# A hybrid decoder trunk on one core: another order of work in the state-space scans, and of the output projection and the way into the last feed-forward block

## What is computed

```python
proj = u @ w_in                       # z (2048 columns), x/B/C (3072), dt (32)
xbc = silu(causal_depthwise_conv(xbc, conv_w, conv_b))
y = ssd_chunked(xs, dt, A, Bm, Cm) + xs * D       # 4 groups of 8 heads, 8 chunks of 128 tokens
y = y * silu(z)
yg = y.reshape(b, s, 4, 512)
yg = yg * rsqrt(mean(yg * yg, axis=-1) + EPS)     # one RMS norm per group
x = x + (yg.reshape(b, s, 2048) * norm_w) @ w_out
x = x + swiglu(rmsnorm(x, ffn_norm_w[1]), ...)    # silu(h @ w_gate) * (h @ w_up) @ w_down
x = rmsnorm(x, final_norm_w)
```

## Time and profile before

| | |
|---|---|
| median of 3 runs | 2369.83 us (2365.24 to 2371.79) |
| the profiled execution: device time / span | 2368.59 / 2366.9 us |
| PE busy | 2267.5 us (96%) |
| DVE, ACT, POOL busy | 1425.3, 1146.5, 1373.0 us (60, 48, 58%) |
| DMA | 317.16 MB, mean 134 GB/s |
| mean granted TensorE clock | 0.982 of full speed |

### The profile page before, as it was taken

One profiled execution on the slowest core, in us unless ns is written; L12 is line 12 of the kernel. 1 busy time (PEld: TensorE's weight loads), 2 busy tenths in 40 slices (PEclk: granted clock), 3 DMA queues, 4 the chain that ended last, 5 costly groups with the idle time before them and its releaser, 6 DMA issues.

```text
span 2366.9 us, 29286 instructions
## 1 busy us (share of the span) xinstructions
PE 2267.5 (96%) x10602; PEld 1841.8 (78%) x10602; DVE 1425.3 (60%) x1828; ACT 1146.5 (48%) x2101; POOL 1373.0 (58%) x992
## 2 busy tenths in 40 slices
PE   8999999999999999999999889779979999999998
PEld 6876888888888878888777667558768888888887
DVE  7366754333346888745578778658873424335787
ACT  4056643333334447555588767424643333333445
POOL 3234288777765654877344434235568777774654
PEclk9999999999999999999999989889999999999999
DMA  5110233232339653333444534476323233227844
GB/s 158 54 27 19 107 99 119 85 116 85 116 111 329 206 163 116 107 107 117 137 134 134 179 133 143 165 251 187 126 73 121 98 116 116 85 98 248 268 150 157
DMA packets 193787, 317.16 MB, mean 134 GB/s; under 512 B 21696, under 2 KB 106604, under 8 KB 191084
## 3 DMA queue, kind: packets, MB, share of 16 engines
q1 hardware_dynamic: 191212, 307.55, 38.6%
q10 hardware_dynamic: 2432, 7.73, 0.8%
HBM read 230.68 MB, written 84.56 MB: 133 GB/s over the span
## 4 chain that ended last, share of the span: by engine, by line
PE 84%; DVE 7%; DMA 3%; issue 2%; POOL 2%; SPq 1%; ACT 1%; DVEq 0%; ACTq 0%; POOLq 0%
PE ps L2525 42%; PE ps L2228 5%; PE ps L2230 5%; PE ps L2229 5%; PE ps L2617 5%; PE ps L2621 5%; PE ps L2613 5%; PE ps L2909 1%; PE ps L2913 1%; PE ps L2905 1%; PE ps L2251 1%; PE ps L2974 1%; PE ps L2694 1%; DMA bc_rows<-conv_rows 1%; PE ps L2957 1%
## 5 line engine op out<-in xcount | busy, mean ns | idle before, releaser
L1274 POOL TENSOR_TENSOR s_lo<-s_val,s_hi 128x512 fp32r<-128x512 f32 x154 | 236.1, 1539 | 197.3 <-ACT s_hi L1863 196.7
L3279 DVE TENSOR_TENSOR xres<-ps,xres 128x512 f32<-128x512 f32 x132 | 90.6, 688 | 407.5 <-PE ps L2525 407.5
L1172 POOL TENSOR_TENSOR p_lo<-p_val,p_hi 128x512 fp32r<-128x512 f32 x176 | 240.1, 1374 | 48.8 <-ACT p_hi L1616 43.3
L1616 ACT ACTIVATE p_hi<-p_val 128x512 fp32r<-128x512 f32 x176 | 111.0, 632 | 310.8 <-POOL p_val L1202 310.8
L1143 POOL TENSOR_TENSOR w_lo<-w_raw,w_hi 128x1024 fp32r<-128x1024 f32 x34 | 81.5, 2401 | 195.4 <-ACT w_hi L1471 108.7
L2525 PE MATMUL ps<-xn_hi,p_hi 128*128 128x512 f32 x704 | 190.8, 393 | 1.9 <-ACT xres L1765 1.3
L2525 PE MATMUL ps<-xn_lo,p_hi 128*128 128x512 f32 x704 | 188.8, 390 | 1.4 <-DVE xn_lo L3145 1.4
L2525 PE MATMUL ps<-xn_hi,p_lo 128*128 128x512 f32 x704 | 188.2, 389 | 0.0
L1863 ACT ACTIVATE s_hi<-s_val 128x512 fp32r<-128x512 f32 x154 | 96.9, 629 | 149.1 <-DMA d_val<-in_w_down 86.9
L2228 PE MATMUL ps<-xn_hi,w_hi 128*128 128x512 f32 x400 | 162.1, 405 | 0.0
L2229 PE MATMUL ps<-xn_lo,w_hi 128*128 128x512 f32 x400 | 157.2, 393 | 0.0
(11 more groups left out here) (385 smaller groups left out, 5680.0 us busy)
## 6 DMA issues: line engine op xcount, KB each, us to landing
s_val<-hidden SPq DMA_DIRECT2D x154, 256.0 KB, 2.9
hidden<-xres SPq DMA_DIRECT2D x20, 1792.0 KB, 6.5
wv_g<-in_w_gate SPq DMA_DIRECT2D x22, 1024.0 KB, 5.2
wv_u<-in_w_up SPq DMA_DIRECT2D x20, 1024.0 KB, 5.2
d_val<-in_w_down SPq DMA_DIRECT2D x70, 256.0 KB, 4.0
rows_v<-in_w_down SPq DMA_DIRECT2D x64, 256.0 KB, 3.7
mdec<-decay_sums SPq DMA_DIRECT2D x32, 512.0 KB, 3.9
os_val<-gated_y SPq DMA_DIRECT2D x56, 256.0 KB, 2.8
```

The source lines that it names most:

```text
L1172: pool.tensor_tensor(p_lo[n][:, :, :], src, f(p_hi[n][:, :, :]), ALU.subtract).then_inc(p_lo_done, 1)
L1274: pool.tensor_tensor(s_lo[i][:, :], s_val[i][:, :], f(s_hi[i][:, :]), ALU.subtract)\
L1616: act.activation(p_hi[n][:, :, :], src, ACT.Copy).then_inc(p_hi_done, 1)
```

## The change

- **Scans.** On DVE the rests of the group before stand between `masked_decay(c)` and `token_major(k + 1)`, where they stood behind `token_major`; their chunks are others, and the sums of squares come from POOL to DVE (`square_adds`, 3 instructions in place of 3). POOL takes `w_lo` in halves, at places tied to `cb_full`. `root` and `root_row` of half 0 stand in chunk 7 of the same group (before: chunk 0 of the next), those of half 1 in chunk 3 (before: 4). SP issues `load_bc(g + 1, 0)` in chunk 4 or 5 and `load_xrows(g + 1, 0)` in chunk 5 (before: both in 6, behind stores), `load_xrows(g, 1)` in chunk 0 of g itself. SiLU is spread over the chunks 3, 5, 7 and 1. The last group takes z in pairs and then two threes.
- **Projection.** Eleven slices need nothing of the last group's rests (before: nine); of them SP loads slices 0 to 5 within the scans (before: 0 and 1), with `root_row` ahead of `load_out(3)`. The stores and loads behind them are in a new order. The y side's rests of slices 0 and 1 are DVE's, of 2 to 55 POOL's as before. The 16 additions of M1 to x all stand ahead of the rest of slice 16.
- **Into the FFN.** M7's additions, `make`, `second_T` and `lo` come up to three slices earlier, and the parts of the tail are interleaved otherwise.

```diff
-        OUT_SEQ = ([(0, p) for p in range(6)] + [(1, p) for p in range(3)] + [(0, p) for p in (6, 7)]
-                   + [(1, p) for p in range(3, NO)] + [(j, p) for j in range(2, 7) for p in range(NO)])
+        OUT_SEQ = ([(0, p) for p in range(6)] + [(1, p) for p in range(5)] + [(0, p) for p in (6, 7)]
+                   + [(1, p) for p in range(5, NO)] + [(j, p) for j in range(2, 7) for p in range(NO)])
...
-                         [(0, 1, 2), (3, 4), (5, 6), (7, 8), (9, 10), (11, 12, 13), (14, 15), ()]]
-        SILU_AFTER_CHUNK = [{1: (0, 1), 4: (2, 3, 4)}] + [{2: (0, 1), 4: (2, 3), 6: (4, 5)}] * (G - 1)
-        SILU_LATE = [(5, 6, 7)] + [(6, 7)] * (G - 1)
-        NEXT_PIECE = {6: 0, 7: 1}
-        LATE_PIECE = {0: 2, 1: 3}
+                         [(0, 1), (2, 3), (4, 5), (6, 7), (8, 9), (10, 11, 12), (13, 14, 15), ()]]
+        SILU_AFTER_CHUNK = [{1: (0, 1), 3: (2, 3), 5: (4,), 7: (5,)}]
+        SILU_AFTER_CHUNK += [{3: (0, 1), 5: (2, 3), 7: (4, 5)}] * (G - 2) + [{3: (0, 1), 5: (2, 3), 6: (4,), 7: (5,)}]
+        SILU_LATE = [(6, 7)] * G
...
+        LO_AHEAD = [{1: (2, 0), 2: (3, 0)}] + [{0: (0, 1), 1: (1, 0), 2: (2, 0), 3: (3, 0), 4: (3, 1)}] * (G - 1)
+        LO_BEHIND = [{1: (2, 1), 2: (3, 1)}] + [{1: (1, 1), 2: (2, 1)}] * (G - 1)
+        S_LO_DVE = 2
...
+            def half_lo(piece, half):
+                cols = slice(half * BANK, (half + 1) * BANK)
+                pool.wait_ge(hi_done, piece.count(1))
+                ins = pool.tensor_tensor(w_lo[piece.slot][:, cols], raw[piece.raw][:, cols], f(w_hi[piece.slot][:, cols]),
+                                         ALU.subtract)
...
+            def square_adds(n):
+
+                dve.wait_ge(sq_ready, BG * (n + 1))
+                dve.tensor_tensor(sq[0][:, :], sq[0][:, :], sq[1][:, :], ALU.add).then_inc(sq_added, 1)
+                dve.tensor_tensor(sq[2][:, :], sq[2][:, :], sq[3][:, :], ALU.add).then_inc(sq_added, 1)
+                dve.wait_ge(sq_added, 2 * (n + 1))
+                dve.tensor_tensor(sq[0][:, :], sq[0][:, :], sq[2][:, :], ALU.add).then_inc(sq_summed, 1)
...
                     masked_decay(c)
+                    if c == 0 and g:
+                        for b in range(BG):
+                            row_normed(g - 1, b, 0)
+                    if c == 1 and g:
+                        gated(g - 1, 1)
+                    if c == 2 and g:
+                        square_adds(2 * g - 1)
+                        mixes(g - 1, "S1")
+                    if c == 3 and g:
+                        reciprocal_rms(2 * g - 1)
+                    if c == 4 and g:
+                        for b in H1_ORDER:
+                            row_normed(g - 1, b, 1)
+                    if c == 5:
+                        if g:
+                            mixes(g - 1, "S3")
+                        gated(g, 0)
+                    if c == 6:
+                        square_adds(2 * g)
+                        if g:
+                            mixes(g - 1, "S2")
+                    if c == 7:
+                        reciprocal_rms(2 * g)
+                        if g:
+                            mixes(g - 1, "S4")
                     if k + 1 < NT * G:
                         token_major(k + 1)
-                    if c == 0 and g:
-                        gated(g - 1, 1)
-                        reciprocal_rms(2 * g - 2)
-                    if c == 2 and g:
-                        for b in range(BG):
-                            row_normed(g - 1, b, 0)
...
-                        if (j, p) == (1, 7):
-                            quota, limit = 8, "M1"
-                        elif j >= 2 and p in (0, 1):
-                            quota, limit = (4, "M1") if j == 2 else (0, "M1")
+                        if (j, p) in ((1, 6), (1, 7)):
+                            quota, limit = 4 if p == 6 else 12, "M1"
```

More of the change, by code:

```diff
@@ new lines, in ssd_group @@
+                    if c == 5:
+                        if g:
+                            sp.wait_ge(mix_ready, 8 * q + 4)
+                        else:
+                            for i in range(4):
+                                sp.wait_ge(row_stored[i], 16 * ((len(ROWS) - 1 - i) // 4 + 1))
+                            sp.wait_ge(gc_ready, 1)
+                            load_bc(1, 0)
+                        if not last:
+                            load_xrows(g + 1, 0)
+                        if g:
+                            store_blocks(q, "M7")
@@ L1099, in out_loads @@
+                load_out(15)
+                load_x_back(3)
+                load_x_back(7)
+                for s_ in range(16, OUTS):
                     load_out(s_)
@@ L3216, in second_entry @@
                     taken = 0
[L3217 removed]
+                    for s_ in range(10, OUTS):
                         j, p = OUT_SEQ[s_]
@@ L3257, in second_entry @@
                         tail_b22(i)
-                    for i in range(4):
-                        tail_lo1(i)
+                    make(6)
+                    tail(0)
+                    make(7)
+                    tail(1)
+                    tail(2)
+                    tail_lo1(0)
+                    tail_lo1(1)
+                    tail_t1(3)
+                    tail_t2(3)
+                    tail_lo1(2)
+                    tail_lo1(3)
                     for i in range(4):
```

365 lines of the change are left out of this document (186 added, 179 removed).

## The result

The changed kernel takes **2338.28 us** (median of 4 runs, 2336.78 to 2339.91), the kernel before 2367.53 (4 runs, 2364.37 to 2371.79): ratio **0.9875, 95% interval [0.9856, 0.9895]**. That is 29 us less, where 66 were forecast: less time as said, though by 1.25%, and outside of the range. The profiled execution took 2339.18 us, its span is 2337.2.

The account below looks back on a forecast made before the run. PE was taken as the bound, with about 100 us of losses that an order of work can reach. Gains of 29 + 28 + 4 + 5 = 66 us off 2368.6 gave 2303 us, range 2284 to 2328.

Parts of the forecast that it names:

- Term 1: Scans: earlier input loads end the 20.2 us of `bc_rows` waits, `mdec` waits nearly go; gain 29 us of 34.3 lost.
- I keep 5 us: Scans: 5 us of the 34.3 us loss left in place, for the row's tight round trip and POOL's `xds`.
- it fits by 0.7: Scans, chunks 7 and 3: ydiag through row and `row_normed` to the next `mdec` takes 17.7 us against two chunks' 18.4.
- rival (a): Scans: the row comes late in every group, `rr_rows` taking 6.8 us behind bytes; 18 us back, 2321; chance 0.13.
- Term 2: Projection to slice 16: half 1's row chain costs nothing, smaller waits remain; gain 28 us of 41.8 lost, bounds 18 and 36.
- I add 5: Projection: 5 us allowed for DMA, about 16 MB needed by slice 16 taking 45 us, close to PE's 46.4.
- The clock behind two waits: 3: Projection: 3 us allowed for PE's slower clock after two waits.
- Term 3: Slices 16 to 55: earlier `make` and `second_T` take the idle 3.2 us and a little clock; gain 4 us (2 to 5).
- Into the FFN: Way into the FFN: DVE is the bound; `make`, tails and two late ops interleaved save its idle time; gain 5 us (2 to 9).
- Rival (b): Projection: POOL's rests starve at 4.1 us each while DVE works without a break; 19 us back, 2322; chance 0.12.
- (c): Scans: the wait for inputs stays because `load_xrows` waits for S3; 24 us back, 2327; chance 0.06.
- (d): Scans: DVE becomes the bound, about 99 us per group; 2386 us, slower than before; chance 0.05.

Follow-up runs that it names:

- the versions with all edits: Changed kernel with all follow-up edits except late input loads: rests on VectorE 2303.14 us, rests on POOL 2306.76, rests on VectorE with half 1's row first 2301.90.
- the best versions: Changed kernel with all follow-up edits except late input loads, rests on VectorE: 2303.14 us; same with half 1's row before the early x loads: 2301.90 us.
- the single edit: Changed kernel with the y-side rests of slices 2 to 15 on VectorE instead of POOL: 2335.82 us, ratio 0.9856.
- the combination: Changed kernel with all follow-up edits except late input loads: 2303.14 us with the rests of slices 2 to 15 on VectorE, 2306.76 with them on POOL.

## Why the prediction was wrong

- **Term 1, scans, gain 29, was 21.5.** Its mechanism held: the 20.2 us for `bc_rows` went, and undoing the two loads alone gives 19 us back. It was mis-sized by what "I keep 5 us" left out. The working asked where VectorE's extras would delay `mdec`, and found the 0.7 us; it never asked who else waits for the CB bank. The sums of squares do, and the change put them ahead of both z halves of chunk 2, while VectorE still has the adds and mixes to do: 10.9 us of scans.
- **Term 1 again, the row: "it fits by 0.7" was off.** The row itself came as forecast: in groups 2 and 3 it was usable 8.5 and 8.6 us behind the ydiag (9.1 forecast), and its products took 2.7 (3.3). What failed is "then `cbm` to the next `mdec` 5.3": it was 7.4, for behind the row the four `yx<-yx,gconst,eacs` take 3.87 us in place of 1.14. POOL's `decayed` and `w_lo` run at that time (1408.8 to 1412.4 in group 3), so a collision is likely; in the scans no run tried it. And the two chunks are not 18.4 but 17.6 long, as chunk 0 has no yoff (8.32 us, 1395.41 to 1403.73). So 18.6 stood against 17.6. In group 1, where the chunk before has only one z half, the two chunks are 15.5 long, and the wait was 3.08. PE waited 5.1 us in these three places (3.08, 0.95, 1.06), and moving the row's products gave 5.9 us of scans, a third of rival (a)'s price. But (a)'s mechanism, a row held up behind bytes, did not happen: `rr_rows` took 2.6 to 2.8 us in the scans, not 6.8. The short chunk 0 also helps to show why the working's own 286.4 us, with every chunk at 3.79, was some 3 us too high: the versions with all edits take 283.
- **Term 2, projection, gain 28, was 12.5.** The chain of half 1 was right (no wait at slices 11 and 12), and slice 3 waited, 4.7 instead of 2.5. The step that failed is "I add 5" for the DMA and 2.5 + 1 for M1's adds: slices 13 to 16 waited 14.0. "The clock behind two waits: 3" failed with it: of the 29.3 us over the working's 46.4, 19.9 are idle and 9.4 the slower clock (0.86 granted), since there were more waits for it to fall behind. Two causes of the waits could be read from the code order: slice 15's low part behind slice 16's DMA, with twelve adds in a row (5.6 us for undoing both), and 2 MB of x among the last loads (5.1). The working held 16 MB against PE's time as if they came in order of need and without gaps. The bound beside it, 21.2 MB at full rate, 60 us, is 7 to 9 us under what the best versions reach (66.8 and 69.1 us from the last ydiag to slice 16's first matmul; 73.0 in the changed kernel); that the transfers hold them there is argued from the DMA shares, not shown.
- **Term 3, slices 16 to 55, gain 4, was a loss of 5.9.** The sign was wrong. The step "`make` and `second_T` earlier take the idle 3.2 us" looked at what got earlier, and not at the cycle that the new place of the squares closes between ACT and VectorE. Shown by the squares one slice later: 8.8 us.
- **Into the FFN, gain 5, was 1.6.** VectorE is the bound there, as said, but T3 of tile 3 as the last of its list made PE wait 12.7 us in one piece, before it could start on anything else. Undoing that gave 3.8 us, what was missing.
- **Rival (b)**, that POOL's rests starve, is refuted as it was put: `os_lo` took 1.46 us in the mean, and PE waited for none. The cost of the collision lay on the other engine: 6.5 us more of VectorE in the two groups shown (8 x 0.425 + 6 x 0.512), and of the whole stretch 1.7 us in the single edit and 4.5 in the combination. The Trainium skill's rule (SBUF — State Buffer, "Who interferes with whom"), that a VectorE instruction with two SBUF inputs and a GpSimd one that reads SBUF lock each other out, agrees with this trace, and so does its other half: VectorE's adds from PSUM, with one SBUF input, take 680 ns with POOL at work or not.
- Rivals (c) and (d) did not happen: no wait for inputs, and VectorE was busy for 248.6 of 299.3 us.
- **The range** was narrower than its own terms. Their lowest gains (14, 18, 2 and 2) sum to 36, which is 2333, and the range ended at 2328. Only the scans stayed within their bounds.
